# Second layer's modulation tiles moved from the x expert stream into the convolution, whose taps alternate between two blocks

## What is computed

```python
mx = split(silu(c) @ mod_w[i] + mod_b[i], 6)          # modulation: shift, scale, gate, twice
mc = split(silu(c_ctx) @ mod_w[i] + mod_b[i], 6)
ax = rmsnorm(hx) * (1 + mx[1]) + mx[0]
# layer 1, for x and for the context:
p = h @ w_in                                          # 1024 x 4096, and 32 columns of gates
qkv = silu(conv5(p[..., :3 * D], conv_w))             # depthwise over 5 tokens
... chunked delta rule, gate z, h + mx[2] * (o @ w_out)
# both layers: 128 of 16384 experts for each token
hx = hx + mx[5] * sum(gate * gelu(u[e] . x) * v[e])
```

## Time and profile before

| | |
|---|---|
| median of 3 runs | 2756.65 us (2753.71 to 2761.71) |
| the profiled execution | 2753.88 us, its span 2751.9 us |
| busy: TensorE, VectorE | 2225.0 us (81%), 1928.4 us (70%) |
| busy: ScalarE, GpSimd | 1075.8 us (39%), 920.6 us (33%) |
| HBM read | 919.83 MB, 335 GB/s over the span |
| mean granted TensorE clock | 0.974 |

### The profile page before, as it was taken

One profiled execution on the slowest core, in us unless ns is written; L12 is line 12 of the kernel. 1 busy time (PEld: TensorE's weight loads), 2 busy tenths in 40 slices (PEclk: granted clock), 3 DMA queues, 4 the chain that ended last, 5 costly groups with the idle time before them and its releaser, 6 DMA issues.

```text
span 2751.9 us, 34094 instructions
## 1 busy us (share of the span) xinstructions
PE 2225.0 (81%) x11070; PEld 1183.7 (43%) x11070; DVE 1928.4 (70%) x5170; ACT 1075.8 (39%) x2999; POOL 920.6 (33%) x855
## 2 busy tenths in 40 slices
PE   8889877777777997777777899989978987777777
PEld 4645322222224553222222389977775542222222
DVE  5777887778766677777767477576566776776675
ACT  5544433333333443333333355311334443343433
POOL 0033343333431333333333357101213333333332
PEclk9999999999999999999999999999989999999999
DMA  8499999999996999999999835100029999999997
GB/s 324 160 418 414 403 417 421 420 415 414 407 421 256 418 416 409 421 420 409 413 420 414 339 123 165 43 2 3 24 101 377 392 407 421 421 421 418 415 417 295
DMA packets 142244, 922.96 MB, mean 335 GB/s; under 512 B 16416, under 2 KB 16576, under 8 KB 42880
## 3 DMA queue, kind: packets, MB, share of 16 engines
q0 software_dynamic: 111552, 809.64, 71.5%
q1 hardware_dynamic: 30528, 111.31, 10.8%
HBM read 919.83 MB, written 1.06 MB: 335 GB/s over the span
## 4 chain that ended last, share of the span: by engine, by line
DMA 41%; PE 28%; DVE 15%; issue 8%; ACT 6%; POOL 2%; DVEq 0%; SPq 0%; POOLq 0%; ACTq 0%
DMA buf<-in_experts,buf 37%; PE pY L1732 13%; DVE buf L1100 6%; PE pY L1806 3%; DMA g<-in_mod_tiles 2%; PE pS L1806 2%; ACT buf L576 2%; PE pG L1806 2%; ACT buf L598 1%; POOL lo L1533 1%; PE pS L1659 1%; PE pS L1660 1%; PE pS L1661 1%; DVE g L1108 1%; PE pY L1659 1%
## 5 line engine op out<-in xcount | busy, mean ns | idle before, releaser
L1732 PE MATMUL pY<-buf 128*128 128x512 f32 x3072 | 1511.9, 622 | 442.7 <-ACT buf L598 437.8
L1514 POOL DMA_INDIRECT buf<-in_experts,buf x768 | 763.4, 994 | 1356.5 <-PE pY L1732 1255.3
L1732 PEld LDWEIGHTS pY<-buf 128*128 128x128 f32 x3072 | 538.0, 192 | 1374.3 <-ACT buf L598 967.5
L1100 DVE SCALAR_TENSOR_TENSOR buf<-pS,buf 128x1024 f32<-128x1024 f32 x384 | 470.0, 1224 | 275.5 <-DMA buf<-in_experts,buf 270.0
L592 ACT ACTIVATE buf<-buf 128x1 f32<-128x1 f32 x768 | 155.1, 202 | 1207.5 <-DVE buf L1100 1207.4
L1100 DVE SCALAR_TENSOR_TENSOR buf<-pG,buf 128x1024 f32<-128x1024 f32 x384 | 467.3, 1223 | 183.7 <-DMA buf<-in_experts,buf 178.8
L576 ACT ACTIVATE buf<-ident,buf 128x128 f32<-128x128 f32 x768 | 296.5, 386 | 0.0
L598 ACT ACTIVATE buf<-buf 128x128 f32<-128x128 f32 x768 | 296.4, 386 | 0.1
L1533 POOL TENSOR_TENSOR lo<-raw,hi 128x1024 fp32r<-128x1024 f32 x48 | 116.1, 2429 | 139.1 <-ACT hi L545 138.9
L1659 PE MATMUL pS<-h_hi,hi 128*128 128x256 f32 x480 | 153.5, 320 | 8.9 <-DVE h_lo L1473 6.0
L1660 PE MATMUL pS<-h_lo,hi 128*128 128x256 f32 x480 | 137.6, 287 | 0.0
(11 more groups left out here) (280 smaller groups left out, 2440.8 us busy)
## 6 DMA issues: line engine op xcount, KB each, us to landing
raw<-in_blocks SPq DMA_DIRECT2D x104, 512.0 KB, 3.6
g<-in_mod_tiles SPq DMA_DIRECT2D x56, 512.0 KB, 7.9
buf<-in_experts,buf POOLq DMA_INDIRECT x768, 10.6
raw<-in_mod_wT SPq DMA_DIRECT2D x20, 512.0 KB, 8.8
buf<-in_mod_wT SPq DMA_DIRECT2D x20, 512.0 KB, 8.3
buf<-in_window SPq DMA_DIRECT2D x2, 1024.0 KB, 11.4
buf<-in_keysT POOLq DMA_DIRECT2D x2, 1024.0 KB, 5.5
buf<-in_ctxT SPq DMA_DIRECT2D x1, 1024.0 KB, 10.2
```

Source lines behind the costliest of these rows:

```text
L1100: v.scalar_tensor_tensor(x, h_tok[NT * i // NPICK], 1.0, x, ALU.mult, ALU.mult, accum_out=dots[:, i:i + 1]).then_inc(dotted, 1)
L1514: g_.indirect_dma_start(rows_uv[n % ROW_RING].rearrange("p a d -> p (a d)"), None, table, bass.IndirectOffsetOnAxis(expert[:, i:i + 1].bit ...
L1732: mm = t_.matmul(pY[:, 2 * r + hf, :], diags[:, i % DIAG_RING], rows_uv[n % ROW_RING][:, 1, GRP * hf:GRP * hf + GRP], start=(k == 0), stop ...
```

## The change

The 30 tiles leave stream 1. SyncE now writes out the convolution's loads one by one (`stream_conv`): it waits until the x stream's rows have been used, loads three tiles, then four weight blocks and three tiles in turn, ten times three in all. The tiles go to six buffers where the stream's rows and the context's residual had been. The seventh and later tiles wait for their buffer. VectorE's `conv_section` takes eight blocks a trip in pairs whose taps alternate, each waiting for the last instruction but one (`wait_but_one`), and multiplies 2, 1, 2 and 1 tiles after the four pairs. GpSimd loads the broadcast row `c_late` (512 KB) for that. Bias and scale of these columns are added after the last section in place of the stream's end.

```diff
-MOD_TILES = (26, 30, 0)
+MOD_TILES = (26, 30)
+MOD_TRIP = 3
...
+        late_tiles = [region(b, (D,)) for b in (64, 68, 72, 76, 116, 120)]
+        late_sums = region(110, (MOD_TILES[1],))
+        c_late = region(112, (D,))
...
+            def wait_but_one(self):
+                self.eng.wait_ge(self.s, (self.n if self.base is None else self.i * self.per + self.n) - 1)
...
+            def late_mods(trip):
+
+                for j in range(MOD_TRIP):
+                    k = MOD_TRIP * trip + j
+                    if k >= len(late_tiles):
+                        sp.wait_ge(mod_tile_used, MOD_TILES[0] + k - len(late_tiles) + 1)
+                    sp.dma_start(late_tiles[k % len(late_tiles)], a["mod_tiles"][MOD_TILES[0] + k]).then_inc(mod_in[k % len(late_tiles)], 16)
+
+            def stream_conv():
+
+                sp.wait_ge(row_used, 2 * NPICK)
+                late_mods(0)
+                for trip in range(1, (NKV + 3 * HEADS) // RING):
+                    b = RING * trip
+                    for j in range(RING):
+                        sp.wait_ge(lo_ready, KD + b + j + 1)
+                        sp.dma_start(raw[j][:, :, :], a["blocks"][(W_IN + HEADS + b if b < NKV else W_IN + b - NKV) + j]).then_inc(raw_in[j], 16)
+                    late_mods(trip)
...
-                    if g == 1 and r in (9, 12, 15) and 0 <= 3 * (i // TOPK - 3) + r // 3 - 3 < MOD_TILES[1]:
-                        mod_dot(3 * (i // TOPK - 3) + r // 3 - 3, 0, u + 1)
...
-                with ve.Fori(0, nb // RING) as n:
-                    ch.loop(n, RING * 3)
-                    for j in range(RING):
-                        ve.wait_ge(tap_first, RING * n + (c0 + j + 1))
+                with ve.Fori(0, nb // (2 * RING)) as n:
+                    ch.loop(n, 2 * RING * 3)
+                    for p in range(RING):
                         for i in (0, 1, 3, 4):
...
+                            for j in (2 * p, 2 * p + 1):
+                                if i == 0:
+                                    ve.wait_ge(tap_first, 2 * RING * n + (c0 + j + 1))
+                                elif i == 4 and j % 2:
+                                    ch.wait()
+                                else:
+                                    ch.wait_but_one()
...
+                        for k in ((0, 1), (2,), (3, 4), (5,))[p]:
+                            ve.wait_ge(mod_in[k], 16 * n + 16 * (front_rounds + c0 // (2 * RING) + 1))
+                            v.scalar_tensor_tensor(late_tiles[k], late_tiles[k], 1.0, c_late, ALU.mult, ALU.mult,
+                                                   accum_out=late_sums[:, bass.ds(2 * MOD_TRIP * n + (MOD_TRIP * c0 // RING + k), 1)]).then_inc(mod_tile_used, 1)
...
+            pool.dma_start(c_late, a["c_row"][0:1, :].to_broadcast([P, D])).then_inc(c_late_in, 16)
```

More of the change, by code:

```diff
@@ L357, in build @@
         consts2_in = sem("consts2_in")
+        c_late_in = sem("c_late_in")
         ab_mm = sem("ab_mm")
@@ L483, in stream, with stream_mods @@
                                      .rearrange("o p c e -> p (o c) e")).then_inc(raw_in[j], 16)
[L485 to L491, removed]
+            def stream_mods():
+                sp.wait_ge(scores_done, HEADS)
+                with sp.Fori(0, MOD_TILES[0]) as i:
+                    sp.wait_ge(mod_tile_used, i)
+                    sp.dma_start(mod_tile, a["mod_tiles"][bass.ds(i, 1)].rearrange("o p d -> p (o d)")).then_inc(mod_tile_in, 16)
+            def late_mods(trip):
[13 more added lines that the diff above has]
+                    late_mods(trip)
             sp.wait_ge(mod_lo, FRONT_GRP * RING)
@@ L495, in _ @@
             stream(L0, 0, RING)
-            stream_mods(0)
+            stream_mods()
             stream(L0 + RING, RING, NQ - RING)
             stream(KD, W_IN + HEADS, RING)
-            stream_mods(1)
-            stream(KD + RING, W_IN + HEADS + RING, NKV - RING)
-            stream(KD + NKV, W_IN, NIN)
+            stream_conv()
+            stream(KD + NKV + 3 * HEADS, W_IN + 3 * HEADS, HEADS)
             stream(KD + NKV + NIN, W_OUT, NC)
@@ L1053, in sparse_peer @@
                 u0, n0 = NT * HEADS * g, NPICK * g
-                tile0 = sum(MOD_TILES[:g])
-                columns = (2, 1, 0)[g]
                 def q_low(j):
@@ L1141, in sparse_peer @@
                         mod_dot(2 * (i // TOPK - 3) + r // 12, (r - 9) % 5, u + 1)
-                    if g == 1 and r in (9, 12, 15) and 0 <= 3 * (i // TOPK - 3) + r // 3 - 3 < MOD_TILES[1]:
-                        mod_dot(3 * (i // TOPK - 3) + r // 3 - 3, 0, u + 1)
[L1144 to L1157, removed]
+                if g == 0:
+                    nt = MOD_TILES[0]
+                    ve.wait_ge(mod_tile_used, nt)
+                    mods_add(0, 5 * NC, 6 * NC, mod_sums[:, 0:2 * NC])
+                    mods_add(1, 0, nt - NC, mod_sums[:, 2 * NC:2 * nt])
+                    ve.wait_ge(mod_ready, 5)
+                    mods_scale(1, 0)
                 ve.wait_ge(row_used, NPICK * (g + 1))
@@ L1192, in conv_section @@
-                        ins.then_inc(evacuated, 1)
-                    ch.end(nb // RING)
+                            for j in (2 * p, 2 * p + 1):
[5 more added lines that the diff above has]
+                                    ch.wait_but_one()
+                                t0, t1 = max(0, 2 - i), min(T, T + 2 - i)
+                                o = dst[:, bass.ds(2 * RING * n + j, 1), t0:t1].rearrange("p o t -> p (o t)")
+                                ins = v.scalar_tensor_tensor(o, pY[:, j % RING, t0 + i - 2:t1 + i - 2], cw[:, i, bass.ds(2 * RING * n + (w0 + j), 1)],
+                                                             o, ALU.mult, ALU.add)
+                                if i < 4:
+                                    ch.mark(ins)
+                                else:
+                                    ins.then_inc(evacuated, 1)
@@ L1227, in _ @@
             conv_section(NKV + 2 * RING, 2 * RING, conv_x[:, 2 * RING:], 3 * HEADS - 2 * RING)
+            ve.wait_ge(mod_tile_used, sum(MOD_TILES))
+            m0 = NMOD - MOD_TILES[1]
+            v.tensor_tensor(mods[:, 1, m0:NMOD, 0], late_sums, small[:, NMOD + m0:2 * NMOD], ALU.add).then_inc(mod_ready, 1)
+            ve.wait_ge(mod_ready, 6)
+            scale = mods[:, 1, 4 * NC:5 * NC, 0]
+            link(v.scalar_tensor_tensor(scale, scale, 1.0, small[:, 96 + 3 * NC:96 + 4 * NC], ALU.add, ALU.mult))
             ve.wait_ge(logs_in, 1)
@@ L1522, in _ @@
                 pool.dma_start(dst, src).then_inc(consts2_in, 16)
-            pool.wait_ge(mod_tile_used, sum(MOD_TILES))
+            pool.dma_start(c_late, a["c_row"][0:1, :].to_broadcast([P, D])).then_inc(c_late_in, 16)
+            pool.wait_ge(mod_tile_used, MOD_TILES[0])
             pool.dma_start(masks[:, 0:5 * P + 17 * CH], a["masks"]).then_inc(consts2_in, 16)
```

15 lines of the change are left out of this document (6 added, 9 removed).

## The result

The changed kernel takes 2741.06 us (median of 6 runs, 2734.62 to 2742.57) where the kernel before takes 2755.7 (6 runs on the same chip, 2752.55 to 2761.71): a ratio of 0.9944, 95% interval 0.9931 to 0.9956. That is faster by 0.56%, 15 us. The profiled execution took 2742.57 us, its span 2740.8, against 2751.9 before; the mean granted clock is 0.973.

What follows compares the result with a forecast made beforehand. DMA bytes bound the x stream; in the convolution VectorE, TensorE and GpSimd are nearly full, tied by four PSUM banks. From the 2756.65 us median, -39 + 26 = -13 gave 2743.7 us, range 2721 to 2758.

Steps and rivals of the forecast that it cites:

- What is removed: First layer's x stream, bound by DMA bytes: thirty tiles leave at 1.31 us each, 39 us gained, bounds 38 and 41.
- The pace of a pair: Convolution taps on VectorE: two alternating blocks take 3.2 us in place of 4.7, so 40 blocks need 64 us.
- The price of a product: Tile products on VectorE take turns with GpSimd's splits: 2.1 us each, between 1.25 and 3.7, 63 us for thirty.
- The four stretches of taps: VectorE's convolution stretches, 105.5 us before, become 127: +21.5, less 1.3 for products partly beside a wait.
- The end: Convolution's end: first z block starts 2.6 us later through pairing, plus 2.8 for TensorE's lower clock after a stall.
- The convolution as a whole: All that the convolution pays for taking tiles and products: 26 us, bounds 5 and 74.
- nothing collides: First rival: products run beside GpSimd's splits in the convolution, only the end costs 5 us; 2722 us, chance 0.18.
- the pay without collisions: Convolution with no product meeting a split: VectorE's 101.5 us fit into 105.5, only the end costs, 5 us.
- What costs nothing: Convolution: 30 more loads fit beside 42 of weights; closing modulation instructions move to a 13.9 us VectorE wait, uncovered 0.4.
- The sum: Whole kernel: -39 + 26 = -13, giving 2743.7 us against the median; forecast chance 0.60.
- Turns nearly every time: Second rival, slower: convolution products wait for splits nearly always; break-even 2.5 us a product, 2771 at 3.0; chance 0.12.
- A late queue: Third rival, no change: on SyncE's queue tiles waiting for products delay weight blocks, +8 to 12, about 2753; chance 0.10.

Runs made afterwards that it cites:

- chained taps on constants: Kernel before with its convolution sections written as ten calls of four blocks, taps still chained, waits on constants instead of register values: 2751.12 us, ratio 0.9993.
- the row in PSUM: Changed kernel with c_late copied by VectorE into an idle PSUM tile, so products read one operand from SBUF and one from PSUM: 2730.59 us, ratio 0.9917.
- Without products: Changed kernel with tile loads kept and each product replaced by a memset of one column: 2723.76 us, ratio 0.9887.
- Alternation alone: Kernel before with taps in alternating pairs, no products in the convolution, tiles left in the x stream: 2763.5 us, ratio 1.003.
- taps chained again: Changed kernel with each block's four taps in a row, every one waiting for the last: 2742.85 us, ratio 0.9964.
- The fastest kernels of the study: Changed kernel with c_late copied to PSUM by ScalarE and each eight blocks' last pair chained, 2714.6 us, ratio 0.9862; variants with one-trip last section 2717.76, all pairs chained 2716.89.

## Why the prediction was right

The forecast was 2743.7 us, the time is 2741.06: faster, by the named mechanism, and inside its own range. By its steps:

- **What is removed.** The term was -39 us; the copy at the x stream's end came 38.75 earlier and 158 rows took 402 us, 1.01 of DMA before and after. Right, and not by the luck of one trace: in the ten traces without tiles in the stream that copy stands between 1529.99 and 1541.53 us, at 1534.95 in the mean, and in the three with them between 1573.05 and 1574.66, at 1573.86. The difference is 38.9.
- **The pace of a pair.** Forecast 3.2 us, measured 3.20. Right, and beside the point: "the 40 blocks need 64 us of VectorE" is true, but VectorE wasn't what set the pace. With chained taps on constants (2.04 us a block) the yardstick moved by 0.7 us.
- **The price of a product.** Forecast 2.1 us with a spread from 1.25 to 3.7; measured 2.18, from 1.21 to 3.42. Right, and the cause is shown by the row in PSUM. The Trainium skill ("SBUF — State Buffer", Who interferes with whom) gives the lock between a VectorE instruction with two SBUF inputs and a GpSimd instruction that reads SBUF; this form of product obeys it, 2.18 us with two and 1.21 with one, which no row of before could show. The layout had strict turns, in which a second product always waits. In the trace some second products wait (1.55, then 3.42) and some don't (2.66, then 1.21), and the mean came out nearly the same.
- **The four stretches of taps.** Forecast +20.2 us (+21.5 less 1.3), measured +18.1: they last 24.5, 23.2, 28.7 and 47.2, together 123.6 against 105.5. The end, forecast +5.4, measured +4.6: from the last tap to the table 18.5 us, where it was 13.9.
- **The convolution as a whole.** Forecast +26, measured +23.0. But the two parts of that term were both wrong. It said: 5 us if nothing collides, 21 for the collisions. Without products the kernel pays 10.1; with the row in PSUM, in which no product collides, it pays 12.6, and the products' collisions add 10.4. So the sum came near by luck in part: one half was 5 to 8 us too small, the other 8 to 11 too large. **The step that failed is the pay without collisions**, "64 + 37.5 = 101.5 would still fit" with only the end on top. It compared VectorE's work with the stretches' length and left out when banks come free, and what the operations between the stretches take when they meet a split. Alternation alone costs 9.5 us, with TensorE's waits for taps at 12.4 us against 6.4. Of that the end is 4.4, near the 5.4 it was priced at. The rest, ahead of the last tap, had no price: a pair gives up both banks at its end, and a gate operation met a split (+2.2, there as in the kernel without products); their shares stay open. Why the collisions were priced too dear is argued and not tested: part of the longer products lies where VectorE had waited for a centre tap, 15.1 us of such waits with the row in PSUM, 7.4 in the changed kernel.
- **What costs nothing.** The loads: ratio 0.9887 with and 0.9888 without them, and 0.8 us of waiting for products. Right. The closing instructions on the modulations: the wait before the table is 16.90 us, so they are covered.
- **The sum.** -39 + 26 = -13 was forecast; the first table came 15.8 us earlier and the span is 11.1 shorter. The 4.7 us between the two went after the table: 13.3 us are left at the key load of the second layer's routing and 12.4 at its first gather. That is a matter of single traces. The part behind the table lasts 1019.9 us in this trace, the longest of all, but 1014.2 in the mean of the ten kernels with the tiles out of the stream, and 1013.0 in the mean of the three others. The profiled execution was also the slowest of its six (2742.57 us). By the medians the gain is 14.6 us, against 15.8 at the first table.

The rivals: nothing collides, no (with the row in PSUM its condition holds for the products, and the time is 2730.59 and not 2722). Turns nearly every time, no: 2.18 us a product is below its break-even of 2.5. A late queue, no: the changed kernel's loads waited 0.8 us for products, and ScalarE never for a load.

## What to carry to other kernels

When a loop is fed through a few banks, count when each bank comes free and not only the engine's work: interleaving two blocks made VectorE faster and the kernel 0.3% slower by itself. Work moved from a DMA-bound stream under a convolution still pays if its operands are placed so that it doesn't exclude GpSimd: one operand in PSUM was worth 10.4 us here, and chaining the last pair, with its products ahead of it, another 7.6, in a trace in which the gate operations had come clear of the splits as well. Look at the small operations between the loops too: the same five rows took from 1.22 to 9.32 us here, by what GpSimd did beside them. The fastest kernels of the study, at 0.986 of the time before, gain 2.5 times what the change did.

## What the runs showed of the hardware

- **A wait on a register's value between two dependent VectorE instructions costs 0.16 us more than one on a constant.** Taps of 0.48 us stand 0.66 us apart by the first and 0.50 by the second, in the same kernel (taps chained again) and between two kernels (the one before, and the same in ten calls). The idle time that the rows of before put down to the last tap was mostly not the dependency. The taps' addresses change to constants along with the waits, and no run separates the two; but eight alternating taps take 3.20 us in the changed kernel's last section too, where the addresses come from registers.
- **Independent taps stand 0.39 us apart, dependent ones 0.50**: the rest of the gap, 0.11 us, is what alternation can win a tap once the waits are on constants.
- **The exclusion runs both ways and has no fixed order.** Split and product both grow (2.44 to 2.70 us and 1.21 to 2.18); two small operations of 128x128 that take 0.28 us took 2.49 and 2.33 beside splits. It isn't limited to two SBUF inputs: a TENSOR_SCALAR of 128x128 with one took 2.45 us in place of 0.23 (alternation alone), and a COPY of 128x32 took 2.29 in place of 0.18 (the kernel before).
